# Four edits to the start and the MoE tails of a two-layer encoder kernel: surplus blocks in groups of five, v weights requested ahead of the gathers, first x tile and first weights loaded first, transposes inside the products

## The chip, the cores and the metric

One core of a Trainium2 chip runs the whole kernel. The metric is the device time of one execution in microseconds (us), the median over several executions. Engines are named PE (TensorE), DVE (VectorE), ACT (ScalarE), POOL (GpSimd) and SP (SyncE, which here only issues DMAs); "PEld" is the weight load that goes with each matmul.

## What is computed

Two post-norm layers over x of 512 tokens by 1024 columns, all in float32. Layer 0 mixes with retention and a gated recurrence, layer 1 with HGRN2 heads. After each mixer and after each mixture of experts (MoE) there is a layer norm.

```python
for layer in range(2):
    y = even_mixer(h) if layer == 0 else odd_mixer(h)
    h = layer_norm(ALPHA * h + y)
    y = moe(h)          # 16 experts, 4 groups; each token: best group, its top 2 experts
    h = layer_norm(ALPHA * h + y)
def expert(xb, e):
    return (silu(xb @ w_gate[e]) * (xb @ w_up[e])) @ w_down[e]
```

The reference is dropless: however many tokens choose an expert, all of them are served.

## The kernel before, in words

Every engine has its program written out by hand, and the engines meet at semaphores. A float32 matmul with 512 columns is two PE instructions in the profile.

**Start (layer 0, first input projection).** SP asks for the identity `sq`, then the four 128-token tiles of x (L282), the first 512 columns of `w_in_even` in two halves (L286, L287), and the other four groups (L289). PE runs four warming matmuls (`spin`), transposes the four tiles of x (`turn_h(0, t)`, L425; 8 transposes each), spins three more times, and waits for all of `hT`. ACT copies the transposed tiles to `hT` (L846) after it has issued its own loads, the last of them the retention decay table of 1.8 MB (L866). Then come 20 products `project(n)` (L460) of 16 instructions each. Products 0 to 3 multiply token tile n by the first weight group, so product n needs only tile n. DVE's first work is the rotary step of product 0 (L1105), which waits for all tables.

**MoE.** Each expert has 96 slots, which gives 12 units of 128 rows (`NU`); unit 11 is `LAST`. Tokens beyond 96 go to surplus blocks of 128 rows; their number `nx` comes out of the router (table entry `T_NX`) and can be 0 to 10 (`MAXX`). The weights of three experts are held at a time, in `W[0:12288]`, `W[12288:24576]` and `S[0:12288]`. The results of all units but the last go to DRAM (`slot_rows`). After the last unit each engine runs its surplus loop (PE L638, DVE L1431, ACT, SP):

```python
with pe.Fori(0, MAXX, 1) as j:
    with pe.If(j < nx):
        turn_rows(0, ...); gate_up_extra(...); turn_hidden(...); down_extra(...)
```

POOL gathers each token's two result rows back from DRAM once the last store has landed (L1578, 8 gathers of 128 rows into `Yg`). DVE adds them into `h` (L1253, L1255, the "merges", two per token tile), and PE adds the rows of the last unit in PSUM (L651 with the identity, L656 with a selection matrix, eight instructions per token tile). DVE then normalises tile by tile (L1227 to L1237, `standardise`). In layer 0 the first norm result is transposed (L425), and the v products of layer 1 follow (L702). Their weights, 4 MB, are asked for at L362 once the last up product is done, because they go to `W[12288:20480]`, where expert 14's weights lie. In layer 1 the output is stored after the norm.

Of the kernel before, what the change touches and what calls it, by code (L numbers as in the profile page):

```python
# [15 lines left out]
ALU = mybir.AluOpType  # L16
# [3 lines left out]
P = 128  # L20
# [16 lines left out]
LAST = NU - 1  # L37
ALPHA = float((2.0 * DEPTH) ** 0.25)
# [32 lines left out]
def encoder_kernel(nc, x, w_in_even, w_out_even, lru_conv_w, lru_conv_b, lru_gate_w, lru_gate_b,  # L71
# [3 lines left out]
    with ExitStack() as ctx:  # L75
# [68 lines left out]
        w_v1, w_out1 = W3(12288, ND, D), S3(0, ND, D)  # L144
# [20 lines left out]
        Yg = [S3(0, NT * 2, D), W3(12288, NT * 2, D)]  # L165
# [27 lines left out]
        T_NX, T_STORES, T_COPIES = 10, 11, 12  # L193
# [85 lines left out]
        def _(sp):  # L279
            sp.dma_start(sq[:], c_sq.rearrange("p (a n) -> p a n", a=3)).then_inc(sq_in, 16)  # L280
            for t in range(NT):
                sp.dma_start(h[:, t, :], x[0, t * P:(t + 1) * P, :]).then_inc(x_in[t], 16)  # L282
            for n, first in enumerate(W_GROUPS):
                src = w_in_even[0][:, first:first + 512].rearrange(rows, p=P)
                if n == 0:
                    sp.dma_start(w_grp[0][:, 0:4, :], src[:, 0:4, :]).then_inc(win_in[5], 16)  # L286
                    sp.dma_start(w_grp[0][:, 4:8, :], src[:, 4:8, :]).then_inc(win_in[0], 16)  # L287
                else:
                    sp.dma_start(w_grp[n], src).then_inc(win_in[n], 16)  # L289
            sp.dma_start(gate_w, lru_gate_w[0].rearrange("z g n c d -> c (z g n) d")).then_inc(gatew_in, 16)  # L290
# [43 lines left out]
            def moe_loads(L):  # L334
# [25 lines left out]
                if L == 0:  # L360
                    sp.wait_ge(up_mm[0], NU)
                    sp.dma_start(w_v1, w_in_odd[0][:, D:2 * D].rearrange(rows, p=P)).then_inc(wout_in, 16)  # L362
                sp.wait_ge(table_done, L + 1)
                nx = sp.value_load(tbl[0:1, T_NX:T_NX + 1], min_val=0, max_val=MAXX)
                with sp.Fori(0, MAXX, 1) as j:
                    with sp.If(j < nx):
                        e = sp.value_load(tbl[0:1, bass.ds(j, 1)], min_val=0, max_val=NE - 1)
                        sp.wait_ge(down_mm[L], (j + NU) * 2)
                        load_rows(L, j + NU, 0)
                        load_expert(L, e, 0)  # L370
# [21 lines left out]
            head_weights(0, 0)  # L392
            head_weights(1, 1)
            sp.wait_ge(v_ps, 2 * NT)
            sp.dma_start(masks, c_masks).then_inc(masks_in, 16)
# [20 lines left out]
        def _(pe):  # L416
            def turn_h(n, t):
# [5 lines left out]
                for half in range(2):  # L423
                    for c in range(4):
                        last = pe.transpose(ps[:, 2 * t + half, c * P:(c + 1) * P],  # L425
# [9 lines left out]
            spin(7, 4)  # L435
            for t in range(NT):
                turn_h(0, t)
            pe.wait_ge(hT_done, 2)
            spin(0, 3)
            pe.wait_ge(hT_done, 2 * NT)  # L440

            def project(n):
# [8 lines left out]
                elif n >= 4:  # L451
                    pe.wait_ge(proj_used, n - 3)
                for c in range(ND):
# [1184 lines left out]
```

## Time and profile before

| what | value |
|---|---|
| runs | 1399.14, 1404.2, 1405.28 us; median 1404.2 us |
| the profiled execution, its own time | 1403.62 us |
| its span | 1401.7 us |
| PE busy | 1349.4 us, 96% of the span |
| DVE, ACT, POOL busy | 518.4, 194.1, 166.7 us |
| mean granted PE clock | 0.986 of full |

The profiled execution lies 0.6 us below the median. "Busy" counts an engine's compute instructions and nothing that its sequencer does, so an engine in an empty loop shows as idle. The granted clock is given as a share of full speed: 1.00 is 2.4 GHz and 0.50 is 1.2 GHz. In the rows below "[5.26 <-DVE h L1255]" means that the engine had stood idle for 5.26 us, and what the profile takes to be the releaser.

### The profile page before, as it was taken

The page shows a single profiled execution, that of the slowest core. Times are in us where ns is not written, and L with a number is a line of the kernel's source. Part 1 is how long each engine was busy: PE and PEld are TensorE (multiplying, and loading weights), DVE is VectorE, ACT ScalarE, POOL GpSimd, SP SyncE. Part 2 cuts the span into 40 slices and gives each one's busy share as a digit, 9 for nine tenths or more (in the row PEclk, how much of TensorE's full clock was granted, in tenths as well). Part 3 has the DMA queues.
Part 4 walks back from the last instruction along what each step waited for, and adds up shares of the span by engine and source line. Part 5 has one row for each costly group of instructions (what it writes and reads, how often), then busy time and mean ns, then how long its engine had stood idle before and what let it go on. Part 6 is the DMA issues. An engine that isn't in the chain of part 4 may idle for free.

```text
span 1401.7 us, 16406 instructions
## 1 busy us (share of the span) xinstructions
PE 1349.4 (96%) x6751; PEld 612.8 (44%) x6751; DVE 518.4 (37%) x972; ACT 194.1 (14%) x327; POOL 166.7 (12%) x126
## 2 busy tenths in 40 slices
PE   8999999999999999799999999999999999999995
PEld 4444464633333333244455555555545333333322
DVE  1244763333111111430355666665545131111107
ACT  1025400100000001010211111111111000000000
POOL 0000400050000000200122332222201400000020
PEclk9999999999999999899999999999999999999998
DMA  9920165368999995633421122200085889999852
GB/s 348 353 85 1 45 255 209 155 233 298 408 424 403 425 414 232 249 90 97 127 61 30 31 60 60 60 0 0 21 369 214 295 336 424 406 427 408 372 213 88
DMA packets 82888, 305.75 MB, mean 218 GB/s; under 512 B 5444, under 2 KB 49800, under 8 KB 70408
## 3 DMA queue, kind: packets, MB, share of 16 engines
q1 hardware_dynamic: 61728, 262.81, 48.3%
q10 hardware_dynamic: 16488, 25.21, 4.9%
q0 software_dynamic: 4608, 16.78, 3.2%
q8 instruction: 52, 0.85, 0.2%
q14 instruction: 12, 0.10, 0.0%
HBM read 271.23 MB, written 33.55 MB: 217 GB/s over the span
## 4 chain that ended last, share of the span: by engine, by line
PE 86%; DVE 9%; issue 2%; ACT 1%; ACTq 1%; DVEq 1%
PE ps L559 24%; PE ps L715 13%; PE ps L594 11%; PE ps L460 8%; PE ps L517 7%; PE ps L702 4%; PE ps L737 3%; PE ps L767 2%; PE ps L544 2%; PE ps L509 1%; DVE S L1469 1%; PE ps L582 1%; PE ps L613 1%; PE ps L755 1%; PE ps L485 1%
## 5 line engine op out<-in xcount | busy, mean ns | idle before, releaser
L559 PE MATMUL ps<-W,S 128*32 128x512 f32 (+1 forms) x2048 | 336.7, 596 | 2.3 <-DVE S L1398 2.3
L715 PE MATMUL ps<-hT,W 128*128 128x512 f32 x512 | 232.5, 593 | 0.7 <-ACT W L846 0.7
L559 PE MATMUL ps<-S 128*64 128x512 f32 (+1 forms) x512 | 224.8, 597 | 0.4 <-DVE S L1398 0.4
L594 PE MATMUL ps<-W,hT 128*32 128x512 f32 (+1 forms) x1024 | 172.8, 601 | 1.1 <-DVE hT L1412 1.0
L559 PEld LDWEIGHTS ps<-W,S 128*32 128x32 f32 (+1 forms) x2048 | 97.8, 114 | 148.0 <-issue 143.7
L715 PEld LDWEIGHTS ps<-hT,W 128*128 128x128 f32 x512 | 92.8, 191 | 90.4 <-issue 88.5
L594 PE MATMUL ps<-S,hT 128*32 128x512 f32 (+1 forms) x256 | 113.2, 594 | 1.1 <-DVE hT L1412 1.0
L846 ACT ACTIVATE hT<-ps 128x512 f32<-128x512 f32 x82 | 46.6, 599 | 388.0 <-PE ps L594 287.0
L559 PEld LDWEIGHTS ps<-S 128*64 128x64 f32 (+1 forms) x512 | 62.1, 124 | 71.9 <-issue 70.5
L1600 POOL TENSOR_TENSOR W<-S,sq 128x256 f32<-128x256 f32 x64 | 73.6, 1150 | 160.9 <-PE ps L737 117.2
L460 PE MATMUL ps<-W,hT 128*128 128x512 f32 x192 | 83.0, 593 | 0.7 <-ACT hT L846 0.7
L594 PEld LDWEIGHTS ps<-W,hT 128*32 128x32 f32 (+1 forms) x1024 | 48.8, 114 | 71.5 <-issue 69.7
L1403 DVE TENSOR_TENSOR hT<-hT,ps 128x512 f32<-128x512 f32 x24 | 16.5, 688 | 159.4 <-ACT hT L959 159.4
L737 PEld LDWEIGHTS ps<-S,W 128*128 128x128 f32 x448 | 61.5, 192 | 30.7 <-issue 30.7
L1511 DVE TENSOR_TENSOR S<-S 128x512 f32<-128x512 f32 x64 | 47.8, 748 | 69.9 <-PE ps L737 58.1
L1408 DVE TENSOR_TENSOR hT<-hT,ps 128x512 f32<-128x512 f32 x24 | 16.5, 688 | 149.5 <-PE ps L559 149.5
L1412 DVE COPY hT<-ps 128x512 f32<-128x512 f32 x24 | 16.6, 691 | 137.9 <-PE ps L582 137.9
L737 PE MATMUL ps<-S,W 128*128 128x128 f32 x448 | 63.5, 285 | 1.4 <-issue 0.8
L517 PE MATMUL ps<-S 128*128 128x512 f32 x128 | 58.4, 601 | 1.0 <-DVE S L1447 1.0
L846 ACT ACTIVATE W<-ps 128x512 f32<-128x512 f32 x56 | 32.6, 597 | 174.3 <-PE ps L746 46.8
L460 PEld LDWEIGHTS ps<-W,hT 128*128 128x128 f32 x192 | 36.3, 190 | 46.3 <-issue 45.0
L517 PE MATMUL ps<-W,hT 128*128 128x512 f32 x128 | 55.7, 593 | 0.8 <-ACT hT L846 0.8
(233 smaller groups left out, 1360.9 us busy)
## 6 DMA issues: line engine op xcount, KB each, us to landing
W<-moe_w_gate SPq DMA_DIRECT2D x24, 2048.0 KB, 12.3
W<-moe_w_up SPq DMA_DIRECT2D x24, 2048.0 KB, 13.1
W<-moe_w_down SPq DMA_DIRECT2D x24, 2048.0 KB, 11.5
S<-moe_w_gate SPq DMA_DIRECT2D x8, 2048.0 KB, 13.3
S<-moe_w_up SPq DMA_DIRECT2D x8, 2048.0 KB, 14.2
S<-moe_w_down SPq DMA_DIRECT2D x8, 2048.0 KB, 16.9
W<-w_in_odd SPq DMA_DIRECT2D x32, 512.0 KB, 6.3
slot_rows<-S ACTq DMA_DIRECT2D x4, 2816.0 KB, 19.4
```

Source lines behind the costliest of these rows:

```text
L460: last = pe.matmul(ps[:, 4 + n % 4, :], a, b, start=(c == 0), stop=(c == ND - 1))
L517: last = pe.matmul(ps[:, k, :], srcT[:, c, t * P:(t + 1) * P], w[:, c, half * 512:(half + 1) * 512], start=(start and c == tiles[0]), stop ...
L544: last = pe.transpose(ps[:, 4 + half, c * P:(c + 1) * P], block[:, half * 4 + c:D:ND], ident)
L559: last = pe.matmul(ps[a:a + n, bank, :], xgT[:, c, a:a + n], w[L][slot_of(e)][:, c, :], start=(c == 0), stop=(c == ND - 1))
L594: last = pe.matmul(ps[a:a + n, 2 + half, :], hidT[:, c, a:a + n], wd[L][slot_of(e)][:, c, half * 512:(half + 1) * 512], start=(c == 0), st ...
L702: last = pe.matmul(ps[:, k, :], hT[:, c, t * P:(t + 1) * P], w_v1[:, c, (k % 2) * 512:(k % 2 + 1) * 512], start=(c == 0), stop=(c == ND - 1))
L715: last = pe.matmul(ps[:, f % 2, :], ring[slot][:, f, c, :], hT[:, c, :], start=(c == 0), stop=(c == ND - 1))
L737: last = pe.matmul(o, km[level % 2][:, c * P:(c + 1) * P], mixed(Q2, s, c * P, P), start=True, stop=True)
L767: last = pe.matmul(ps[:, 7, :], vh[:, j, :], attn[:, j, :], start=(j == 0), stop=(j == NT - 1))
L846: return nc.scalar.activation(o, i, ACT.Copy)
L1511: v.tensor_tensor(q, q, view(src, at + 1, [[2, n], [step - 1, 2], [0, s]]), ALU.mult).then_inc(updated, 1)
L1600: pool.tensor_tensor(view(km[level % 2], s, [[4 * s, m], [s, 2], [1, s]]), view(K2, s, [[4 * s, m], [T + s, 2], [1, s]]), view(ones, 0, [[ ...
```

## The change

1. The surplus blocks come in up to two groups (`ROUNDS`) of five (`PER_ROUND`). The table holds the number of groups that are needed: 0, 1 or 2. Each engine's loop goes twice over the groups, with one test per group, and inside it five times over the blocks with none. A group that is needed at all runs all five blocks.
2. The v weights go to `S[0:8192]`, where expert 13's gate and up weights lie, and are asked for after the up product of unit 10 rather than unit 11. The gathered rows of layer 0 move to the down part of `S` and to `W[0:4096]`. The masks of layer 1 are asked for a little earlier.
3. SP asks for x tile 0, then both halves of the first weights, then x tiles 1 to 3, then weight group 1, then the decay table (which leaves ACT's queue), then the rest.
4. PE spins once rather than seven times. The transposes of tiles 1 to 3 stand inside products 0 to 2, after their fifth of eight steps. DVE copies them to `hT` instead of ACT.

```diff
 NU = NE * CAP // P
 MAXX = 2 * T // (CAP + 1)
 LAST = NU - 1
+ROUNDS = 2
+PER_ROUND = MAXX // ROUNDS
 ALPHA = float((2.0 * DEPTH) ** 0.25)
 LN_EPS, RMS_EPS = 1e-5, 1e-6
 GELU_C = 2.0 * float(np.sqrt(2.0 / np.pi))
...
-        w_v1, w_out1 = W3(12288, ND, D), S3(0, ND, D)
+        w_v1, w_out1 = S3(0, ND, D), S3(0, ND, D)
...
-        Yg = [S3(0, NT * 2, D), W3(12288, NT * 2, D)]
+        Yg = [[S3(8192, NT, D), W3(0, NT, D)], [W3(12288, NT, D), W3(16384, NT, D)]]
...
-        T_NX, T_STORES, T_COPIES = 10, 11, 12
+        T_ROUNDS, T_STORES, T_COPIES = 10, 11, 12
...
+
+            def rows_in(t):
                 sp.dma_start(h[:, t, :], x[0, t * P:(t + 1) * P, :]).then_inc(x_in[t], 16)
+
+            rows_in(0)
             for n, first in enumerate(W_GROUPS):
                 src = w_in_even[0][:, first:first + 512].rearrange(rows, p=P)
                 if n == 0:
                     sp.dma_start(w_grp[0][:, 0:4, :], src[:, 0:4, :]).then_inc(win_in[5], 16)
                     sp.dma_start(w_grp[0][:, 4:8, :], src[:, 4:8, :]).then_inc(win_in[0], 16)
+                    for t in range(1, NT):
+                        rows_in(t)
                 else:
                     sp.dma_start(w_grp[n], src).then_inc(win_in[n], 16)
+                if n == 1:
+                    sp.dma_start(decay, c_decay).then_inc(tab_in, 16)
             sp.dma_start(gate_w, lru_gate_w[0].rearrange("z g n c d -> c (z g n) d")).then_inc(gatew_in, 16)
             sp.wait_ge(proj, 20)
             sp.dma_start(w_out0, w_out_even[0].rearrange(rows, p=P)).then_inc(wout_in, 16)
...
                 if L == 0:
-                    sp.wait_ge(up_mm[0], NU)
+                    sp.wait_ge(up_mm[0], LAST)
                     sp.dma_start(w_v1, w_in_odd[0][:, D:2 * D].rearrange(rows, p=P)).then_inc(wout_in, 16)
                 sp.wait_ge(table_done, L + 1)
-                nx = sp.value_load(tbl[0:1, T_NX:T_NX + 1], min_val=0, max_val=MAXX)
-                with sp.Fori(0, MAXX, 1) as j:
-                    with sp.If(j < nx):
-                        e = sp.value_load(tbl[0:1, bass.ds(j, 1)], min_val=0, max_val=NE - 1)
-                        sp.wait_ge(down_mm[L], (j + NU) * 2)
-                        load_rows(L, j + NU, 0)
-                        load_expert(L, e, 0)
+                rounds = sp.value_load(tbl[0:1, T_ROUNDS:T_ROUNDS + 1], min_val=0, max_val=ROUNDS)
+                with sp.Fori(0, ROUNDS, 1) as r:
+                    with sp.If(r < rounds):
+                        with sp.Fori(0, PER_ROUND, 1) as i:
+                            j = r * PER_ROUND + i
+                            e = sp.value_load(tbl[0:1, bass.ds(j, 1)], min_val=0, max_val=NE - 1)
+                            sp.wait_ge(down_mm[L], (j + NU) * 2)
+                            load_rows(L, j + NU, 0)
+                            load_expert(L, e, 0)
 
 
             sp.wait_ge(lru_done, 1)
...
             head_weights(0, 0)
+            sp.dma_start(masks, c_masks).then_inc(masks_in, 16)
             head_weights(1, 1)
             sp.wait_ge(v_ps, 2 * NT)
-            sp.dma_start(masks, c_masks).then_inc(masks_in, 16)
...
-                        last = pe.transpose(ps[:, 2 * t + half, c * P:(c + 1) * P],
+                        last = pe.transpose(ps[:, (2 * t + half) % (4 if n == 0 else 8), c * P:(c + 1) * P],
...
             pe.wait_ge(sq_in, 16)
-            spin(7, 4)
-            for t in range(NT):
-                turn_h(0, t)
-            pe.wait_ge(hT_done, 2)
-            spin(0, 3)
-            pe.wait_ge(hT_done, 2 * NT)
+            spin(7, 1)
+            turn_h(0, 0)
 
             def project(n):
 
...
                     pe.wait_ge(proj_used, n - 3)
+                if n < NT:
+                    pe.wait_ge(hT_done, 2 * n + 2)
                 for c in range(ND):
                     if n == 0 and c == 4:
                         pe.wait_ge(win_in[0], 16)
+                    if n < NT - 1 and c == 5:
+                        turn_h(0, n + 1)
...
                 pe.wait_ge(table_done, L + 1)
-                nx = pe.value_load(tbl[0:1, T_NX:T_NX + 1], min_val=0, max_val=MAXX)
+                rounds = pe.value_load(tbl[0:1, T_ROUNDS:T_ROUNDS + 1], min_val=0, max_val=ROUNDS)
                 copies = pe.value_load(tbl[0:1, T_COPIES:T_COPIES + 1], min_val=2 * NU, max_val=2 * (NU + MAXX))
                 turn_hidden(LAST)
                 down(LAST)
-                with pe.Fori(0, MAXX, 1) as j:
-                    with pe.If(j < nx):
-                        turn_rows(0, (j + NU // 3) * 16)
-                        gate_up_extra(j + NU, (j + NE // 2 + 1) * 16)
-                        turn_hidden(j + NU)
-                        down_extra(j + NU, (j + NE // 2 + 1) * 16)
+                with pe.Fori(0, ROUNDS, 1) as r:
+                    with pe.If(r < rounds):
+                        with pe.Fori(0, PER_ROUND, 1) as i:
+                            j = r * PER_ROUND + i
+                            turn_rows(0, (j + NU // 3) * 16)
+                            gate_up_extra(j + NU, (j + NE // 2 + 1) * 16)
+                            turn_hidden(j + NU)
+                            down_extra(j + NU, (j + NE // 2 + 1) * 16)
 
...
-            act.dma_start(decay, c_decay).then_inc(tab_in, 16)
-            for t in range(NT):
-                turn_copies(0, t)
...
+            for k in range(2 * NT):
+                dve.wait_ge(hT_ps, k + 1)
+                v.tensor_copy(hT[:, 4 * (k % 2):4 * (k % 2) + 4, (k // 2) * P:(k // 2 + 1) * P],
+                              ps[:, k % 4, :].rearrange("p (c n) -> p c n", c=4)).then_inc(hT_done, 1)
...
-                    done(v.scalar_tensor_tensor(h[:, t, :], Yg[L][:, 2 * t, :], gts[:, t, 0:1], h[:, t, :],
+                    done(v.scalar_tensor_tensor(h[:, t, :], Yg[L][t // 2][:, 2 * (t % 2), :], gts[:, t, 0:1], h[:, t, :],
-                    v.scalar_tensor_tensor(h[:, t, :], Yg[L][:, 2 * t + 1, :], gts[:, t, 1:2], h[:, t, :],
+                    v.scalar_tensor_tensor(h[:, t, :], Yg[L][t // 2][:, 2 * (t % 2) + 1, :], gts[:, t, 1:2], h[:, t, :],
...
-                v.tensor_copy(r_tb[0:1, T_NX:T_NX + 1], r_end[0:1, NE - 1:NE])
-                done(v.tensor_scalar(r_tb[0:1, T_STORES:T_STORES + 1], r_end[0:1, NE - 1:NE], float(NU // 2), 16.0,
-                                     ALU.add, ALU.mult))
-                done(v.tensor_scalar(r_tb[0:1, T_COPIES:T_COPIES + 1], r_end[0:1, NE - 1:NE], float(NU), 2.0,
-                                     ALU.add, ALU.mult))
+                extra, n = r_end[0:1, NE - 1:NE], r_tb[0:1, T_ROUNDS:T_ROUNDS + 1]
+                done(v.tensor_scalar(n, extra, 1.0, None, ALU.is_ge))
+                for k in range(1, ROUNDS):
+                    done(v.scalar_tensor_tensor(n, extra, float(k * PER_ROUND + 1), n, ALU.is_ge, ALU.add))
+                v.tensor_scalar(r_tb[0:1, T_STORES:T_STORES + 1], n, 16.0 * PER_ROUND, 16.0 * (NU // 2),
+                                ALU.mult, ALU.add)
+                done(v.tensor_scalar(r_tb[0:1, T_COPIES:T_COPIES + 1], n, 2.0 * PER_ROUND, 2.0 * NU,
+                                     ALU.mult, ALU.add))
...
-                        pool.indirect_dma_start(Yg[L][:, 2 * t + k, :], None, xs,
+                        pool.indirect_dma_start(Yg[L][t // 2][:, 2 * (t % 2) + k, :], None, xs,

```

The loops of ACT and DVE are rewritten in the same way as those of SP and PE, around the same calls.

**PE at the start.** The order of PE's instructions before (L432 `spin`, L425 transposes, L460 products):

```order
L432 MATMUL ps<-sq 128x384 [waits sq_in]
L432 MATMUL ps<-sq 128x384 x3
L425 MATMUL ps<-sq,h 128x128 [waits x_in_0]
L425 MATMUL ps<-sq,h 128x128 x7
...
L425 MATMUL ps<-sq,h 128x128 [waits x_in_3]
L425 MATMUL ps<-sq,h 128x128 x7
L432 MATMUL ps<-sq 128x384 [waits hT_copied]
L432 MATMUL ps<-sq 128x384 x2
L460 MATMUL ps<-W,hT 128x512 [waits win_in_5,hT_copied]
L460 MATMUL ps<-W,hT 128x512 x3
L460 MATMUL ps<-W,hT 128x512 [waits win_in_0]
```

And now (the same three are L443, L436 and L471):

```order
L443 MATMUL ps<-sq 128x384 [waits sq_in]
L436 MATMUL ps<-sq,h 128x128 [waits x_in_0]
L436 MATMUL ps<-sq,h 128x128 x3
L471 MATMUL ps<-W,hT 128x512 [waits hT_copied,win_in_5]
L471 MATMUL ps<-W,hT 128x512 x3
L471 MATMUL ps<-W,hT 128x512 [waits win_in_0]
L436 MATMUL ps<-sq,h 128x128 [waits x_in_1]
L436 MATMUL ps<-sq,h 128x128 x7
L471 MATMUL ps<-W,hT 128x512 x3
L471 MATMUL ps<-W,hT 128x512 [waits hT_copied]
```

The first product now waits for tile 0 of x alone, and the transposes of tile 1 stand in it. The list folds repeated rows, so a transposed tile is still eight transposes.

**SP at the start**, before:

```order
L280 DMA sq<-c_sq 128x384
L282 DMA h<-x 128x1024 x4
L286 DMA W<-w_in_even 128x4x512
L287 DMA W<-w_in_even 128x4x512
L289 DMA W<-w_in_even 128x8x512 x4
```

and now:

```order
L282 DMA sq<-c_sq 128x384
L285 DMA h<-x 128x1024
L291 DMA W<-w_in_even 128x4x512
L292 DMA W<-w_in_even 128x4x512
L285 DMA h<-x 128x1024 x3
L296 DMA W<-w_in_even 128x8x512
L298 DMA S<-c_decay 128x3584
L296 DMA W<-w_in_even 128x8x512 x3
```

The first weights have moved ahead of three tiles of x, and the decay table ahead of three weight groups.

**PE at the end of the MoE**, layer 0, before (L594 down product of the last unit, L638 and L639 the loop and its test, then the surplus block):

```order
L594 MATMUL ps<-W,hT 32x512 x31
L638 UNCONDITIONAL_BRANCH
L639 COMPARE_AND_BRANCH
L550 ISA
...
L639 UNCONDITIONAL_BRANCH
L638 REGISTER_ALU
L638 COMPARE_AND_BRANCH
```

and now:

```order
L605 MATMUL ps<-W,hT 32x512 x31
L649 UNCONDITIONAL_BRANCH
L650 COMPARE_AND_BRANCH
L651 UNCONDITIONAL_BRANCH
L651 ISA
...
L651 REGISTER_ALU
L651 COMPARE_AND_BRANCH
L650 UNCONDITIONAL_BRANCH
L649 REGISTER_ALU
L649 COMPARE_AND_BRANCH
L664 MATMUL ps<-h,sq 128x512 [waits rows_merged,first_rows_or_last_sel_copied]
```

The outer loop and its test are of the same form as before, but go round twice rather than ten times. The inner loop (L651) is reached only where the test holds.

## Rows read from the trace of the kernel before

**Rows 1.** Page, part 1: busy time by engine, share, instructions.

```profile
PE 1349.4 (96%) x6751; PEld 612.8 (44%) x6751; DVE 518.4 (37%) x972; ACT 194.1 (14%) x327; POOL 166.7 (12%) x126
```

**Rows 2.** Timeline of the start: start us, length us, engine, line, operation, count.

```profile
3.25 4.42 PE L432 MATMUL ps<-sq 128*128 128x384 f32 x8 [3.25 <-DMA sq<-c_sq]
7.51 3.29 PE L425 MATMUL ps<-sq,h 128*128 128x128 f32 x24
12.18 4.03 ACT L846 ACTIVATE hT<-ps 128x512 f32<-128x512 f32 x8
16.26 27.73 PE L460 MATMUL ps<-W,hT 128*128 128x512 f32 x64 [0.74 <-ACT hT L846]
25.68 0.43 DVE L1105 TENSOR_TENSOR S<-S,rot 128x256 f32<-128x256 f32 x1 [25.68 <-DMA S<-c_decay]
```

**Rows 3.** Chain of waits, a later `spin` with PE at full clock: start us, length us.

```profile
268.50 3.32 PE ps L432 x10
```

**Rows 4.** Line 286 (first half of the first weights): issue, and time to landing.

```profile
L286 SPq DMA_DIRECT2D W<-w_in_even x1: 580/580/580, 3.0 to 3.0; - x1
DMA to landing us min/median/max: 11.3/11.3/11.3
```

**Rows 5.** SP's DMA queue (packets, MB, share), in windows 0 to 8 and 0 to 12.6 us.

```profile
q1 hardware_dynamic: 566, 1.77, 68.5%
q1 hardware_dynamic: 1239, 3.34, 76.3%
```

**Rows 6.** Page, part 6: every load of MoE gate weights.

```profile
W<-moe_w_gate SPq DMA_DIRECT2D x24, 2048.0 KB, 12.3
S<-moe_w_gate SPq DMA_DIRECT2D x8, 2048.0 KB, 13.3
```

**Rows 7.** Timeline of PE, DVE and POOL around layer 0's last unit.

```profile
568.83 8.77 PE L594 MATMUL ps<-W,hT 128*32 128x512 f32 x64 [0.98 <-DVE hT L1412]
582.87 3.75 PE L651 MATMUL ps<-h,sq 128*128 128x512 f32 x4 [5.26 <-DVE h L1255]
600.46 7.10 PE L702 MATMUL ps<-W,hT 128*128 128x512 f32 x16 [0.83 <-ACT hT L846]
...
576.79 1.28 DVE L1253 SCALAR_TENSOR_TENSOR h<-S,gts,h 128x1024 f32<-128x1024 f32 x1 [8.21 <-issue]
586.79 1.28 DVE L1253 SCALAR_TENSOR_TENSOR h<-S,gts,h 128x1024 f32<-128x1024 f32 x1 [2.35 <-DMA S<-slot_rows,dst]
...
562.76 1.03 POOL L1578 DMA_INDIRECT S<-slot_rows,dst  x1 [250.14 <-DMA slot_rows<-hT]
```

**Rows 8.** Chain in the same place: steps of DVE's sequencer in its empty loop.

```profile
571.38 0.71 issue
...
575.29 0.06 DVEq L1432
...
575.82 0.06 DVEq L1432
```

**Rows 9.** Timeline of SP: the issue ahead of the v weights' in its program.

```profile
544.84 0.43 SPq L298 DMA_DIRECT2D S<-ln_b  x1
```

**Rows 10.** Timeline of PE, DVE and POOL around layer 1's last unit.

```profile
1374.44 3.75 PE L651 MATMUL ps<-h,sq 128*128 128x512 f32 x4 [6.13 <-issue]
...
1367.82 1.28 DVE L1253 SCALAR_TENSOR_TENSOR h<-W,gts,h 128x1024 f32<-128x1024 f32 x1 [8.42 <-issue]
1380.22 1.30 DVE L1227 BATCH_NORM_STATS2 sm<-ps 128x6 f32<-128x512 f32 x2 [2.25 <-PE ps L656]
...
1354.81 1.03 POOL L1578 DMA_INDIRECT W<-slot_rows,dst  x1 [249.12 <-DMA slot_rows<-hT]
```

**Rows 11.** Gathers of layer 1: GB/s in 40 slices of 1356 to 1370 us.

```profile
GB/s 0 117 105 105 234 410 433 304 339 328 386 363 374 433 363 199 281 222 328 316 328 339 281 363 339 316 316 351 398 398 339 398 421 433 421 386 316 222 23 0
```

**Rows 12.** Stretches: length, busy us (instructions) of PE, PEld, DVE, ACT, POOL; granted clock; DMA share; GB/s.

```profile
568.80:577.60 8.80, 8.77 (x64) 2.85 (x64) 0.81 (x1) 0.60 (x1) 2.87 (x4) 0.81 1.02 401
582.80:586.60 3.80, 3.73 (x5) 1.70 (x6) 1.60 (x2) 1.28 (x1) 0.00 (x0) 0.50 0.94 376
```

More of the change, by code:

```diff
@@ L865, in _ @@
             act.dma_start(iota[:], c_iota).then_inc(tab_in, 16)
-            act.dma_start(decay, c_decay).then_inc(tab_in, 16)
-            for t in range(NT):
-                turn_copies(0, t)
             def projected(n):
@@ L985, in moe @@
                 act.wait_ge(table_done, L + 1)
-                nx = act.value_load(tbl[0:1, T_NX:T_NX + 1], min_val=0, max_val=MAXX)
-                with act.Fori(0, MAXX, 1) as j:
-                    with act.If(j < nx):
-                        sigmoid(j + NU)
-                        store(j + NU, 0, (j + NU // 2) * 16)
+                rounds = act.value_load(tbl[0:1, T_ROUNDS:T_ROUNDS + 1], min_val=0, max_val=ROUNDS)
+                with act.Fori(0, ROUNDS, 1) as r:
+                    with act.If(r < rounds):
+                        with act.Fori(0, PER_ROUND, 1) as i:
+                            j = r * PER_ROUND + i
+                            sigmoid(j + NU)
+                            store(j + NU, 0, (j + NU // 2) * 16)
             norm_std(0, 0)
@@ L1429, in moe @@
                 dve.wait_ge(table_done, L + 1)
-                nx = dve.value_load(tbl[0:1, T_NX:T_NX + 1], min_val=0, max_val=MAXX)
-                with dve.Fori(0, MAXX, 1) as j:
-                    with dve.If(j < nx):
-                        copy_rows(j + NU)
-                        hidden(j + NU)
-                        copy_hidden(j + NU)
+                rounds = dve.value_load(tbl[0:1, T_ROUNDS:T_ROUNDS + 1], min_val=0, max_val=ROUNDS)
+                with dve.Fori(0, ROUNDS, 1) as r:
+                    with dve.If(r < rounds):
+                        with dve.Fori(0, PER_ROUND, 1) as i:
+                            j = r * PER_ROUND + i
+                            copy_rows(j + NU)
+                            hidden(j + NU)
+                            copy_hidden(j + NU)
             norm_mixer(0)
```

## Prediction

> **What bounds the kernel now.** I began with the busy times: PE computes for 1349.4 of 1401.7 us [rows 1], so all that a change outside PE's own instructions can reach is some 52 us of PE idle time, plus stretches in which PE runs at half clock. The waits, in order of time, put that idle time in a few places. The change touches three of them: the start, and the end of the MoE in each layer. So I read the timeline there.
>
> *Start.* PE's first product begins at 16.26 us, released by ACT's last copy [rows 2]. ACT copies only from 12.18 us, because its own loads stand ahead on its queue. The first half of the weights, which the same product needs, was asked for at 3.05 us and landed 11.3 us later, at 14.35 [rows 4]. So both releasers are within 2 us of each other: a faster copy alone would gain little, and the order of the loads matters.
>
> *End of layer 0's MoE.* The last down product ends at 568.83 + 8.77 = 577.6 us; PE then stands idle for 5.26 us [rows 7]. The profile names DVE's merge as the releaser, but DVE merged tile 0 from 576.79 to 579.4, long before 582.87. What is left is PE's own empty loop. DVE's loop shows what a round costs: its sequencer passes the same line at 575.29 and 575.82, 0.53 us a round [rows 8], and ten rounds are 5.3 us, which is PE's whole gap. Layer 1 shows 6.13 us there [rows 10].
>
> *No surplus block runs.* There are 24 + 8 = 32 loads of gate weights [rows 6], which is 16 experts times 2 layers. Every round of the loops is an empty one.
>
> **The change part by part.**
>
> *Loops.* Ten empty rounds become two of the same form, so 8 x 0.53 = 4.2 us go on PE, and as much on DVE, ACT and SP. In layer 0 PE's gap falls from 5.3 to 1.1 us, and its sums may begin at 578.7 rather than 582.87. What could hold them is the merge. DVE's idle time before its merges was 8.21 us [rows 7]; less 4.2 it is 4.0, so they begin at about 572.6 and take 2.6 us a tile. Tile 0 is merged at 575.2, before PE asks. In layer 1 PE's gap falls from 6.1 to 1.9 us and the merges begin at 1367.82 - 4.2 = 1363.6 [rows 10].
>
> *Clock.* The long gap costs twice. In it the granted clock fell to 0.50, that is 1.2 GHz, and stayed there for the first 3.8 us of the sums [rows 12]: the first tile's eight instructions took 5.4 us, where eight at full clock take 3.4 (27.73 / 64 = 0.43 us each, rows of the products [rows 2]). With a gap of 1.1 us it may stay at 2.4 GHz. The evidence is mixed: gaps of 1.48 and 0.98 us close together brought it to 0.81 on the mean of the down product that followed [rows 12], in layer 1 nothing of the kind shows. So layer 0 gains 4.2 us (clock falls all the same) to 6.1 us (it holds). I take **5.5**.
>
> *Layer 1's end.* PE's last product ends at 1374.44 - 6.13 = 1368.3, and the first sum is ready 5.8 us after PE's start, at 1380.22, which is what DVE's norm waits for [rows 10]; the rest is DVE's chain of four norms, unchanged. After the change the sum begins at 1370.2 and is ready at 1373.6 (full clock) to 1375.9 (half). DVE must have merged all four tiles first: four times 2.6 us from 1363.6 are 1373.8. The gathers bound this too. They begin at 1354.81 and their traffic ends at 1369.3 [rows 10, 11]; with a landing lag of 1.75 us (below) tile 3 is merged at 1373.7. So the norm begins between 1373.8 and 1375.9, a gain of 4.3 to 6.4 us. I take **5.5**, nearer to the full clock since the gap of 1.9 us is nearer to those that hardly lowered it than to 6.1. This is also why faster loops alone can't give more: DVE and the gathers stand right behind.
>
> *v weights earlier.* In layer 0 DVE waited 2.35 us for tile 3's rows, until 586.79 [rows 7], with the v weights on the same DMA engines (share 1.02 [rows 12]). With PE's sums moved up, tile 3's sum would be due at 578.7 + 3 x 3.44 = 589.0, and the merge ended at 589.4; the norm of tile 0, behind that merge on DVE, would end 1.4 us after PE's last sum. Asked for at about 545.3, behind the issue at 544.84 [rows 9], the weights are nearly through when the gathers begin at 562.8, and these then take as long as in layer 1, to about 579. So this edit is worth 0 to 1.4 us, and only because of the first; it is within the 5.5. What it may hurt is queued on the same engines: the last down weights, due at 568.8, and the store of unit 10 before the gathers. 2.1 + 1.0 + 4.2 + 0.5 MB at the 401 GB/s of [rows 12] are 19.5 us, until 564.5, so the store may land 2 to 3 us later. The last merge moves to 585 at most, before 589.0: no cost. The masks, the new places and one more small DVE operation in the table lie beside PE work and are not waited for: nothing.
>
> *Start.* SP's queue had moved 1.77 MB by 8.0 us and 3.34 MB by 12.6 [rows 5]. Before, the first half of the weights had the identity and all of x ahead of it, 0.2 + 2.1 + 1.05 = 3.34 MB; it landed at 14.35, so the lag is 1.75 us. Now it has 0.2 + 0.52 + 1.05 = 1.77 MB and lands at 8.0 + 1.75 = **9.75 us**. Tile 0's transposes and DVE's two copies are done before. The second half and tiles 1 to 3 follow at 0.34 MB a us: 12.9, 14.4, 16, 17.5, each before its use. So the products begin 6.5 us earlier. Two things are given back. The transposes of three tiles now stand on PE's path: 3.29 us for 24 [rows 2]. And the warming goes: the first eight spin instructions took 4.42 us, 0.55 each [rows 2], where ten later ones took 3.32 [rows 3], so PE starts at half rate here. (The clock row says 1.00 at the start, but the durations decide.) One spin and one tile of transposes with idle time between will hardly raise it before 9.75; then the first product pays what the first sum paid, 2.1 us. The gain is 6.5 - 3.3 - 2.1 = **1.1 us**; bounds: 4.0 (weights at 9.0 and full clock) and -1.0 (a tile or half of the weights 2 us late).
>
> The Trainium skill ("TensorE: Matmul & The Clock Gate", part 1) speaks against this edit: PE's default clock is the low one, and work issued before it has been busy for a while runs at half rate, however few instructions it is. By that page the removed spins were no waste, and the start gains 1.1 us rather than 3.2. The durations above agree.
>
> The decay table lands later than DVE's first rotary step at 25.68 us [rows 2], by some 3 us, but PE needs the rotated rows only after product 7, at about 70 us.
>
> **Sum.** 1.1 + 5.5 + 5.5 = 12.1 us off the profiled execution's 1403.6, which is 1391.5; that execution lies 0.6 us under the median, so 1392.0.
>
> **The rivals.**
>
> *The loops' time is not by the round.* DVE's gap of 8.2 us is more than 5.3: four or five steps took 0.7 us each [rows 8], and they may be a fixed price of entering and leaving the loop that PE pays as well. For it: layer 1's gap on PE is 6.1. Against it: layer 0's is 5.3, ten rounds exactly. Then PE's gap falls only to some 3 us, the clock falls too, and each layer gains 2.3: 1404.2 - 1.1 - 4.6 = 1398.5.
> The Trainium skill ("Runtime: NRT & Kernel Launch", Instruction fetch mechanics) says that a taken branch to code outside the fetched window stalls until it is fetched. By it such steps belong to jumps, not to rounds, and would stay; no row here tells which it is.
>
> *All goes well at once.* The start keeps full clock, both first sums too, and the gathers come early: 4.0 + 7 + 7 = 18 us, 1386.
>
> *Slower: groups of five.* A layer with one surplus block now runs five. Place: the end of that MoE, PE's path. Price: a block has 16 + 16 + 16 product instructions at 0.43 us, 21 us, so four needless blocks cost at least 83 us: 1475 or more. It decides as soon as one expert is chosen by more than 96 tokens. [Rows 6] speak against it flatly: neither layer has a surplus block.
>
> **How the numbers follow.** Forecast 0.68 (own range 1388 to 1396); fixed loop price 0.15; all at once 0.13; groups of five 0.02; something else near no change 0.02. 0.5% is 7.0 us, about what a measurement can tell from no change: below 1397.2 is faster. That is the forecast, all at once and a third of the fixed-price case: 0.86. Same takes the rest of that case, 0.12. Slower 0.02. The range runs from 1386 to 1398: both bounds of the unknowns added up give 4.0 + 6.1 + 6.4 = 16.5 and -1.0 + 4.2 + 4.3 = 7.5 us, and 1386 and 1398 take in part of the two rivals.
>
> **What would show it.** First product at 9 to 10.5 us, its first instructions near 0.86 us apart, product 3 ended near 42.6 rather than 43.8. PE idle 1 to 2 us before the identity sums in both layers, granted clock 1.00 in the first sum. v products from 594 to 596. Layer 1's first norm at about 1368 us, 12 earlier than 1380.2. No DMA wait before DVE's last merge. I am wrong if PE's gaps stay over 3 us, if the products at the start wait for tiles of x, or if gathers become the releaser of PE's sums.

## The result, and the profile after the change

The changed kernel takes 1386.85 us in the median (1386.09 to 1388.84, 4 runs), against 1404.14 us before (1399.14 to 1405.28). The ratio is 0.9886, with a 95% interval of 0.986 to 0.9912: 17.3 us, or 1.1%, faster. The prediction said 1392.0 with a range of 1386 to 1398, so the direction is right, the step is 1.4 times the forecast one (17.3 against 12.1 us), and the time lies near the low end of the range. The profiled execution took 1388.84 us, the slowest of the four; its span is 1387.0 us, 14.7 less than before.

PE's own work has hardly changed (page, part 1; compare [rows 1]):

```profile
PE 1346.3 (97%) x6739; PEld 613.2 (44%) x6739; DVE 524.5 (38%) x982; ACT 189.9 (14%) x319; POOL 167.2 (12%) x126
```

*The start.* PE's timeline there, which answers to [rows 2]:

```profile
3.19 1.65 PE L443 MATMUL ps<-sq 128*128 128x384 f32 x2 [3.19 <-DMA sq<-c_sq]
5.34 1.97 PE L436 MATMUL ps<-sq,h 128*128 128x128 f32 x8 [0.50 <-DMA h<-x]
8.57 6.68 PE L471 MATMUL ps<-W,hT 128*128 128x512 f32 x10 [1.25 <-DMA W<-w_in_even]
15.09 1.04 PE L436 MATMUL ps<-sq,h 128*128 128x128 f32 x8
40.95 27.68 PE L471 MATMUL ps<-hT,W 128*128 128x512 f32 x64
```

The first product begins at 8.57 us, released by the weights, and its first ten instructions take until 15.09. At full clock ten take 4.3 us, so the half rate costs 2.2. The granted-clock column reads 1.00 for this stretch, as it did at the start before the change; that PE is at half rate is read from the durations, and the warm start below bears it out. No transpose inside a product waits for x. The second group of products begins at 40.95 us (before: 43.90).

*The end of layer 0's MoE*, PE, POOL and DVE, which answers to [rows 7]:

```profile
565.25 8.77 PE L605 MATMUL ps<-W,hT 128*32 128x512 f32 x64 [0.98 <-DVE hT L1431]
573.95 1.98 PE L664 MATMUL ps<-h,sq 128*128 128x512 f32 x4
589.65 7.11 PE L715 MATMUL ps<-S,hT 128*128 128x512 f32 x16 [0.83 <-ACT hT L859]
...
563.86 1.03 POOL L1599 DMA_INDIRECT S<-slot_rows,dst  x1 [251.18 <-DMA slot_rows<-hT]
...
570.78 1.28 DVE L1269 SCALAR_TENSOR_TENSOR h<-S,gts,h 128x1024 f32<-128x1024 f32 x1 [5.78 <-DMA S<-slot_rows,dst]
```

PE's gap of 5.26 us is gone: the identity sum follows the last down product at once. DVE is through its loop early and now waits for the gathered rows. The granted clock is 0.80 in the down product and 1.00 in the first sum.

*The end of layer 1's MoE*, PE and DVE, which answers to [rows 10]; the last three lines are from the chain of waits:

```profile
1359.71 1.98 PE L664 MATMUL ps<-h,sq 128*128 128x512 f32 x4
...
1354.17 1.29 DVE L1269 SCALAR_TENSOR_TENSOR h<-W,gts,h 128x1024 f32<-128x1024 f32 x1 [1.72 <-DMA W<-slot_rows,dst]
1365.57 1.29 DVE L1243 BATCH_NORM_STATS2 sm<-ps 128x6 f32<-128x512 f32 x2
...
1356.59 6.44 DMA W<-slot_rows,dst
1363.03 0.03 issue
1363.05 1.30 DVE h L1269
```

Here too PE's gap is gone. What ends last now is POOL's eighth gather (6.44 us from issue to landing), then tile 3's merge, then the norms. Before, PE's empty loop stood in that place.

The difference of the two profiled executions, summed up from the start of the same instruction in both:

| place | before | after | gained since the start |
|---|---|---|---|
| second product group begins | 43.90 | 40.95 | 2.95 |
| retention finished, out projection begins | 204.66 | 203.37 | 1.29 |
| layer 0, first-row selection | 289.86 | 288.58 | 1.28 |
| layer 0, last up product | 558.55 | 555.58 | 2.97 |
| v products begin | 600.46 | 589.65 | 10.81 |
| layer 1, first-row selection | 1082.99 | 1074.34 | 8.65 |
| layer 1, DVE behind the last up product | 1357.18 | 1350.23 | 6.95 |
| last norm begins | 1380.22 | 1365.57 | 14.65 |

So the three places that the change touches gave 2.95, 7.84 (10.81 - 2.97) and 7.70 us (14.65 - 6.95), 18.5 in all. The stretches in between, which it does not touch, lost 3.8 us net: 1.7 before the out projection, 2.2 and 1.7 on either side of layer 1's first-row selection, while layer 0's MoE gained 1.7. PE's instructions there are the same. The mean granted clock is 0.01 lower in the three that lost and 0.01 higher in the one that gained, and PE's busy time moves with it (from 43.90 to 204.66 us before, 158.28 us; the same work after, 159.95 us).

### The profile page after: what moved, and what is told of

The parts are those of the page before. It is cut to its first block, busy times and chain, and to the rows that moved or that the text cites. A ratio compares the mean times of both kernels' runs of the same rounds, so it can differ in the third digit from the quotient of the medians.

```text
span 1387.0 us, 16128 instructions
## 1 busy us (share of the span) xinstructions
PE 1346.3 (97%) x6739; PEld 613.2 (44%) x6739; DVE 524.5 (38%) x982; ACT 189.9 (14%) x319; POOL 167.2 (12%) x126
## 4 chain that ended last, share of the span: by engine, by line
PE 88%; DVE 8%; DMA 1%; issue 1%; ACT 1%; POOL 0%; DVEq 0%; POOLq 0%; SPq 0%
PE ps L570 24%; PE ps L728 14%; PE ps L605 12%; PE ps L471 8%; PE ps L528 7%; PE ps L715 4%; PE ps L750 4%; PE ps L780 2%; PE ps L555 2%; PE ps L443 1%; PE ps L520 1%; DVE S L1490 1%; PE ps L593 1%; PE ps L624 1%; PE ps L768 1%
## 5 line engine op out<-in xcount | busy, mean ns | idle before, releaser
L859 ACT ACTIVATE hT<-ps 128x512 f32<-128x512 f32 x74 | 42.5, 596 | 385.9 <-PE ps L605 287.0
L471 PE MATMUL ps<-W,hT 128*128 128x512 f32 x192 | 85.6, 605 | 1.3 <-DMA W<-w_in_even 1.3
L1532 DVE TENSOR_TENSOR S<-S 128x512 f32<-128x512 f32 x64 | 47.8, 747 | 69.9 <-PE ps L750 58.0
L471 PEld LDWEIGHTS ps<-W,hT 128*128 128x128 f32 x192 | 36.9, 195 | 46.5 <-issue 44.8
L715 PE MATMUL ps<-S,hT 128*128 128x512 f32 x128 | 55.7, 593 | 0.8 <-ACT hT L859 0.8
## 6 DMA issues: line engine op xcount, KB each, us to landing
W<-moe_w_gate SPq DMA_DIRECT2D x24, 2048.0 KB, 12.6
```

The costliest lines, as they stand in the source:

```text
L471: last = pe.matmul(ps[:, 4 + n % 4, :], a, b, start=(c == 0), stop=(c == ND - 1))
L715: last = pe.matmul(ps[:, k, :], hT[:, c, t * P:(t + 1) * P], w_v1[:, c, (k % 2) * 512:(k % 2 + 1) * 512], start=(c == 0), stop=(c == ND - 1))
L859: return nc.scalar.activation(o, i, ACT.Copy)
L1532: v.tensor_tensor(q, q, view(src, at + 1, [[2, n], [step - 1, 2], [0, s]]), ALU.mult).then_inc(updated, 1)
```

## The experiments

Each kernel was run beside the kernel before. The theory: an empty round costs every engine 0.53 us, and nothing else; the loads' order and the transposes inside the products need each other; the early v weights matter little. Its rivals: a fixed price of the loops; a single edit that carries the start; v weights that matter.

**Ten groups of one block.**

```diff
-ROUNDS = 2
+ROUNDS = 10
```

> The changed kernel with ten groups of one block, so each empty loop goes round ten times again; all else as changed. If the price is by the round (0.53 us), PE stands idle 5 to 6 us before its identity sums in both layers, the clock falls in that gap, and each layer's end is 6 to 8 us longer than in the changed kernel: 1386.9 + 14 = about 1401. If the price is that of entering and leaving a loop, PE's gap stays near nothing and the time within 2 us of 1387.

Measured: 1397.14 us (1394.55 to 1398.68), ratio 0.9963 (0.9949 to 0.9977). That is 10 us more than the changed kernel, and its gaps are back. PE and DVE at both ends:

```profile
567.07 7.07 PE L605 MATMUL ps<-W,hT 128*32 128x512 f32 x64 [0.98 <-DVE hT L1431]
579.02 3.46 PE L664 MATMUL ps<-h,sq 128*128 128x512 f32 x4 [4.88 <-DVE h L1271]
...
1368.23 3.75 PE L664 MATMUL ps<-h,sq 128*128 128x512 f32 x4 [5.20 <-issue]
1361.10 1.28 DVE L1269 SCALAR_TENSOR_TENSOR h<-W,gts,h 128x1024 f32<-128x1024 f32 x1 [5.39 <-issue]
```

The price is by the round: PE stands for 4.88 and 5.20 us, and the first sum runs at the low clock again (granted 0.53 and 0.50 in it). In layer 0 the profile names DVE's merge as the releaser, but that had ended at 576.03. DVE's 5.39 us in layer 1 are ten rounds at 0.53 with no slow step among them, so a round and its jump can pass without the slow steps of [rows 8]; this nested loop is other code than the loop before, so what brings them is not shown. Entering and leaving the loop is the same here as in the changed kernel, so the rival of a fixed price is out. The total was expected 4 us higher. Layer 1's end is 6.0 us longer than in the changed kernel, as expected; layer 0's, from the last up product to the v products, only 4.7 (38.81 against 34.07), because part of the gap takes the place of time that the changed kernel loses there too: 1.7 us to a low clock in the down product, or 1.7 us of waiting for the first rows (last experiment).

**The two groups of five alone, in the kernel before.** The table of the groups and the loops are taken over, nothing else; for example on PE:

```diff
-                with pe.Fori(0, MAXX, 1) as j:
-                    with pe.If(j < nx):
+                with pe.Fori(0, ROUNDS, 1) as r:
+                    with pe.If(r < rounds):
+                        with pe.Fori(0, PER_ROUND, 1) as i:
```

> The kernel before with the two groups of five alone. By the round: PE's gaps of 5.3 and 6.1 us vanish; layer 1's end gains what it gained in the changed kernel (7.7 us), layer 0's a little less than its 7.8, since the v weights still share the DMA engines with the gathers and DVE's last merge is late: 1404.1 - 14 = 1390, give or take 2 for the clock. Fixed price: 1402 or more.

Measured: 1396.2 us (1393.79 to 1397.01), ratio 0.9952 (0.9938 to 0.9965). Half of what was expected. PE's gaps at the loop are gone, except for 0.65 us in layer 0, but in layer 0 PE now waits for the merges of tiles 1 to 3, and each of these for its gather:

```profile
575.32 1.95 PE L657 MATMUL ps<-h,sq 128*128 128x512 f32 x4 [0.65 <-issue]
579.96 1.98 PE L657 MATMUL ps<-h,sq 128*128 128x512 f32 x4 [0.97 <-DVE h L1263]
585.36 1.98 PE L657 MATMUL ps<-h,sq 128*128 128x512 f32 x4 [1.70 <-DVE h L1263]
590.73 1.98 PE L657 MATMUL ps<-h,sq 128*128 128x512 f32 x4 [1.67 <-DVE h L1263]
...
577.30 1.28 DVE L1261 SCALAR_TENSOR_TENSOR h<-S,gts,h 128x1024 f32<-128x1024 f32 x1 [4.94 <-DMA S<-slot_rows,dst]
588.07 1.29 DVE L1261 SCALAR_TENSOR_TENSOR h<-S,gts,h 128x1024 f32<-128x1024 f32 x1 [2.76 <-DMA S<-slot_rows,dst]
```

Tiles come 5.4 us apart while the v weights share the DMA engines. The faster loop turned one wait into another: from the last up product to the v products it is 39.31 us, only 2.6 less than before. Layer 1's end gained 5.1 us rather than 7.7; in this one profile its last store took 5.5 us to land, with nothing large beside it (DMA share 0.28), and the gathers began that much later. Why is open.

**The changed kernel with late v weights.**

```diff
-                    sp.wait_ge(up_mm[0], LAST)
+                    sp.wait_ge(up_mm[0], NU)
```

> The changed kernel with the v weights asked for after the last up product again, at their new place. If their early start matters now that the loops are short: the gathers of layer 0 take 20 us or more from the first to the last merge's rows instead of 15, the sums or the first transposes behind them wait, and the v products begin 1 to 4 us later against the end of the last down product; 1388 to 1391. If other work hides it: no DMA wait that PE sees, under 0.5 us.

Measured: 1391.33 us (1389.46 to 1393.49), ratio 0.9926 (0.9901 to 0.9952), 4.5 us slower than the changed kernel (on another chip; by the ratios to the kernel before it is 0.4%, 5.6 us). PE's sums and the v products:

```profile
574.90 1.98 PE L664 MATMUL ps<-h,sq 128*128 128x512 f32 x4
578.44 1.88 PE L664 MATMUL ps<-h,sq 128*128 128x512 f32 x4
583.68 1.98 PE L664 MATMUL ps<-h,sq 128*128 128x512 f32 x4 [1.65 <-DVE h L1271]
589.04 1.98 PE L664 MATMUL ps<-h,sq 128*128 128x512 f32 x4 [1.66 <-DVE h L1271]
595.54 7.10 PE L715 MATMUL ps<-S,hT 128*128 128x512 f32 x16 [0.83 <-ACT hT L859]
```

From the first sum to the v products it takes 20.6 us here and 15.7 in the changed kernel: 4.9 us. The first gather, at 560.76 us, is earlier than there, but tile 3's rows come 25.6 us after it, where the changed kernel has them within 15 to 16. The early request is worth that, not the 0 to 1.4 us of the prediction.

**One group of ten.**

```diff
-ROUNDS = 2
+ROUNDS = 1
```

> The changed kernel with one group of ten blocks, so one empty round. If PE's two rounds are already hidden behind the last down product in the array, and DVE waits for gathered rows, nothing is left to gain: gaps as in the changed kernel, 1387 within 2. If each round still shows, 0.5 us less in each layer.

Measured: 1388.62 us (1384.9 to 1389.34), ratio 0.9898 (0.9864 to 0.9932): no difference to the changed kernel. PE's sum in layer 1 begins at once, in layer 0 it waits 1.38 us for DVE's merge, whose rows are late. Two rounds are as good as one: with two, no gap is left on PE that the rounds make.

**The start: x first.**

```diff
-            rows_in(0)
+            for t in range(NT):
+                rows_in(t)
...
-                    for t in range(1, NT):
-                        rows_in(t)
...
-                if n == 1:
-                    sp.dma_start(decay, c_decay).then_inc(tab_in, 16)
...
+            act.dma_start(decay, c_decay).then_inc(tab_in, 16)
```

> The changed kernel with the loads in the old order: all four tiles of x before the weights, the decay table on ACT's queue. If the order of the loads carries the gain at the start: the first product begins at about 14.4 us (where the first half of the weights landed before) and product 3 ends near 46.5, because the transposes stand inside the products and the clock is low; that is 5 to 6 us later than in the changed kernel (40.9) and later than before the change (43.8): about 1392. If moving the transposes and the copies to DVE carries it, product 3 ends by 42.

Measured: 1391.62 us (1390.42 to 1395.19), ratio 0.993 (0.9902 to 0.9957). The first product and the one that ends the first group:

```profile
14.35 6.33 PE L468 MATMUL ps<-W,hT 128*128 128x512 f32 x10 [7.30 <-DMA W<-w_in_even]
...
36.88 9.61 PE L468 MATMUL ps<-W,hT 128*128 128x512 f32 x22
```

It begins at 14.35 us, as expected from [rows 4], and product 3 ends near 46.3, 2.5 us later than before the change. Transposes inside the products, with the spins gone, are a loss by themselves. Most of it is the half rate: the first ten instructions take 6.33 us where 4.3 would do.

**The start: transposes first.**

```diff
-            spin(7, 1)
-            turn_h(0, 0)
+            spin(7, 4)
+            for t in range(NT):
+                if t >= 2:
+                    pe.wait_ge(hT_done, 2 * t - 2)
+                turn_h(0, t)
+            pe.wait_ge(hT_done, 2 * NT)
...
-                    if n < NT - 1 and c == 5:
-                        turn_h(0, n + 1)
```

> The changed kernel with its new order of loads, but four spins and all four transposed tiles ahead of the first product again. If both edits are needed together: tile 3 of x lands at about 16, the first product begins at 18 to 19 and product 3 ends at 45 to 47; about 1392. If the new order of loads alone gives the gain, product 3 ends by 42.

Measured: 1395.08 us (1392.43 to 1399.69), ratio 0.9953 (0.9931 to 0.9975).

```profile
14.07 5.38 PE L436 MATMUL ps<-sq,h 128*128 128x128 f32 x24 [4.12 <-DMA h<-x]
20.24 26.02 PE L473 MATMUL ps<-W,hT 128*128 128x512 f32 x60 [0.78 <-DVE hT L1112]
```

PE waits for tile 1 until 14.07, and the first product begins at 20.24, later than the expected 18 to 19. There is no further wait for x; the 24 transposes behind tile 1 take 5.38 us at a granted clock of 0.50, where 24 took 3.29 before [rows 2]. Product 3 ends at 47.8. The weights ahead of x are a loss by themselves too. Only the pair gains.

**A warm start.**

```diff
-            spin(7, 1)
+            spin(7, 2)
             turn_h(0, 0)
+            spin(7, 1)
```

> The changed kernel with two spins before the first transposes and one behind them, so PE is hardly idle from 3.2 us to the first product. If the 2.1 us lost in the first product (ten instructions in 6.4 us) are the low clock, and it can be raised by then: the first product begins at 8.6 to 9.2 and product 3 ends 1 to 2 us earlier than 40.9; the total gains as much, within the noise of 1387. If the clock stays low whatever is spun, product 3 ends at 40.9 to 41.5.

Measured: 1385.35 us (1384.59 to 1386.27), ratio 0.9875 (0.9851 to 0.9899). The total is within the noise of the changed kernel, the profile is not:

```profile
10.11 4.56 PE L472 MATMUL ps<-W,hT 128*128 128x512 f32 x10 [2.17 <-DMA W<-w_in_even]
```

Ten instructions in 4.56 us where the changed kernel took 6.68: the removed spins had been worth 2.1 us. The expectation still missed: the weights landed 1.5 us later in this execution, so the first product did not begin by 9.2, and product 3 ended at 40.5, hardly before 40.9.

**A warm start, and spins in the wait at the retention scores.**

```diff
             scores(0)
             pe.wait_ge(proj_used, 16)
+            spin(7, 7)
```

> As the one before, and with seven spins in PE's wait of 2.5 us between the first and second head's retention scores, where the clock fell and PE's instructions up to 186 us took 1.7 us longer in the changed kernel than before the change. If idle time lowers the clock there: granted clock 1.00 in that stretch and 1.5 to 3 us off, 1383 to 1385 in all. If the clock falls for another reason: no gain, or a loss of up to 0.5 us where the spins outlast the wait.

Measured: 1382.95 us (1380.37 to 1384.53), ratio 0.9859 (0.9831 to 0.9886). The stretch of 165 to 190 us, first of the changed kernel in its second profile (last experiment), then of this one:

```profile
165.00:190.00 25.00, 22.53 (x64) 11.98 (x62) 16.70 (x24) 2.08 (x3) 1.54 (x1) 0.80 0.84 342
```

```profile
165.00:190.00 25.00, 25.00 (x107) 14.95 (x107) 18.36 (x40) 2.09 (x3) 0.00 (x0) 1.00 0.94 387
```

The granted clock (third from the right) is 1.00 where it was 0.80. In the eleven profiles without these spins, the kernel before included, it is 0.80 or 0.86 in this stretch. So here idle time lowers it, and the idle time can be filled. Seven spins took 4.78 us in a wait of 2.5, so they outlasted it by about 2 us.

**The v weights ahead of the last down weights**, in the changed kernel: the same request, moved up in SP's program to just behind unit 10's up product.

```diff
+                        if L == 0 and u == LAST - 1:
+                            sp.wait_ge(up_mm[0], LAST)
+                            sp.dma_start(w_v1, ...).then_inc(wout_in, 16)
                         next_down(L, q + 3, q)
```

> The changed kernel with the v weights asked for still earlier, as soon as unit 10's up product is done, ahead of expert 15's down weights and the norm's rows. If the slow landing of unit 10's store (7.5 us against 3.5 with the v weights late) is due to those weights on the same DMA engines: the store lands in about 3.5 us and layer 0's first gather begins 3 to 4 us earlier against the last down product. PE's sum then waits for no merge; the total gains 0 to 1.8 us (nothing where the down product ran at the low clock, as in the changed kernel's profile). If the store is slow for another reason: still 7 to 8 us.

Measured: 1384.94 us (1383.58 to 1385.2), ratio 0.9879 (0.9853 to 0.9904). The store of unit 10 and the first gather that waits for it:

```profile
556.49 0.34 ACTq L979 DMA_DIRECT2D slot_rows<-hT  x1
559.97 1.03 POOL L1599 DMA_INDIRECT S<-slot_rows,dst  x1 [248.47 <-DMA slot_rows<-hT]
```

In the changed kernel the same two are

```profile
556.32 0.34 ACTq L979 DMA_DIRECT2D slot_rows<-hT  x1
...
563.86 1.03 POOL L1599 DMA_INDIRECT S<-slot_rows,dst  x1 [251.18 <-DMA slot_rows<-hT]
```

That is 3.48 us here against 7.5 there (8.2 in its second profile). So the v weights, asked for where the change put them, do delay the store by 4 us. Asked for at 533.07 us they land 12.7 us later instead of 22.9, and the store finds the engines at a share of 0.32 (556 to 560 us). PE's sum waits for no merge, though the down product ran at full clock. The median is 2.3 us below that of the changed kernel on the same chip, and the ranges do not overlap.

**Both, with shorter spins.** The last kernel with the warm start, three spins at the scores and one in each of the two short gaps:

```diff
+                spin(4, 1)
                 turn_hidden(LAST)
+                spin(4, 1)
                 down(LAST)
```

> As the one before, with the spins at the start (two and one), three spins in the wait at the retention scores, and one spin in each of the two short gaps ahead of the last down product. If idle gaps lower the clock and the spins fit into them: last down product 7.1 us in both layers, first scores without a dip, no gap before the sums; 1379 to 1382. If the spins in the short gaps delay the down product instead: 1383 or more.

Measured: 1377.73 us (1377.2 to 1383.32), ratio 0.9842 (0.9814 to 0.987), the fastest median of all and below the expected 1379 to 1382: 9.5 us under the changed kernel on the same chip. Its slowest run, 1383.32, is still faster than every run of that. The last down product and the sum of layer 0:

```profile
559.20 7.07 PE L607 MATMUL ps<-W,hT 128*32 128x512 f32 x64 [0.33 <-DVE hT L1435]
566.20 1.98 PE L668 MATMUL ps<-h,sq 128*128 128x512 f32 x4
```

Neither the low clock nor a gap before the sum. The clock in 165 to 190 us is 1.00 here as well, with PE's second scores begun 2.2 us earlier than with seven spins.

**The changed kernel once more**, on the chip of the last two.

> The changed kernel itself, beside the two others on the same chip: 1385 to 1389, ratio to the kernel before 0.986 to 0.990. Its profile tells how much of the clock's dips in the places that the change does not touch differ from one execution to the next; if they do not differ, they follow from the change and not from chance.

Measured: 1387.27 us (1385.31 to 1389.52), ratio 0.9894 (0.987 to 0.9918). In this second profile the first product begins at 9.85 us, the second group at 42.48, and layer 0's last down product takes 7.07 us rather than 8.77 (granted clock 1.00 rather than 0.80). PE then waits for DVE's first merge:

```profile
575.11 1.96 PE L664 MATMUL ps<-h,sq 128*128 128x512 f32 x4 [1.73 <-DVE h L1271]
```

So the end of layer 0's MoE is no shorter for it: 34.23 us from the last up product to the v products, 34.07 in the first profile. The stretch at 165 to 190 us has clock 0.80 as in the first profile. So part of the dips differs from one execution to the next and part comes back each time.

## Why the prediction was right, and where its sizes were off

*Loops.* Right in mechanism: with ten groups PE's gaps of 5 us are back. Mis-sized in two terms. The first: I let the two rounds that remain cost 1.1 us in layer 0 and left a gap of 1.9 us in layer 1. No gap is left in either ("1359.71 ... L664" has none before it). Why the remaining rounds don't show is open; that they run in PE's sequencer while the array still works would fit, but is not shown. The second: of layer 0's 5.5 us the loops were to bring most. With the loops alone (second experiment) that end gained 2.6 us, since the wait for the loop became a wait for rows.

*Clock behind the gap.* Right: the first sum of four instructions takes 1.98 us where it took 3.75, in both layers, at a granted clock of 1.00 where it was 0.50. The shorter gap was worth about 2 us besides the gap itself, in each.

*v weights.* The step that failed is "this edit is worth 0 to 1.4 us". It measured 4.9 us in the profile and 4.5 in the total. I had compared the old landing of tile 3 with sums that began a microsecond late, and had not seen that with the loop shortened PE's sums of the later tiles would each wait for their own gather. So the 7.8 us of layer 0's end, against 5.5 taken, hold two errors of opposite sign: the loops gave less, the v weights more. The cost side was closer: the store was said to land 2 to 3 us later, and landed 4 us later. The prediction called that harmless. It is so only where the last down product runs at the low clock. In the second profile, where it did not, PE waited 1.73 us, and in the runs with one group, with the warm start and with the seven spins 1.4 to 1.8. That is the prediction's own sign of being wrong, gathers as what PE's sums wait for: it showed there, and not in the first profile.

*Layer 1's end.* Taken 5.5 us, bounds 4.3 to 6.4; it gave 7.7, and 8.1 in the second profile, so both lie outside the bounds. The gathers bind, as said, but DVE began its merges at 1354.17, 1.72 us behind its last copy, while I had left it 4.2 us of loop and slow steps. So it was never late, and the norm began 18.2 us after the first gather rather than 19 to 21.

*Start.* Taken 1.1 us; the first profile gave 2.95 and the second 1.4 (43.90 to 42.48). The second group began between 40.73 and 42.77 us in the six profiles with this start, and at 43.90 and 43.27 in the two with the old one. The term that differs most is the landing of the weights: products from 9.75 us predicted, from 8.57 in the first profile, 9.85 in the second. The three tiles of transposes cost 2.6 us rather than 3.3 (15.09 to 15.96 us for the first of them). The low clock's 2.1 us are as predicted (2.2), and the warm start got them back. The Trainium skill ("TensorE: Matmul & The Clock Gate", part 1) says that the throttled clock is PE's default and that activity releases it. The runs agree: ten instructions took 6.68 us behind one spin and 4.56 behind three.

*Rivals.* The fixed price of the loops is refuted by the ten groups. No surplus group ran in any execution, so the price of groups of five was not tried. "All goes well at once", put at 0.13, is nearer to the time (1386) than the forecast (1392), and two of its three parts happened: both ends gave over 7 us with the first sums at full clock. Its start did not: that kept the low clock.

*The sum.* 1.1 + 5.5 + 5.5 = 12.1 us predicted against 17.3 measured in the medians. The three places gave 18.5 us in the profiled execution (17.2 in the second profile), and the stretches elsewhere took 3.8 back (1.4). The time lies inside the stated range, 1386 to 1398, but outside the range of the forecast itself, 1388 to 1396. That it is inside owes something to the room left for the rivals, since each of the three terms was too small.

## What to carry to other kernels

An empty round of a guarded loop is not free: where several engines run ten of them behind the last product, it made the two longest waits of PE in this program (6.13 and 5.26 us), and grouping the rounds removed them. Before you shorten a wait, look up which transfer stands right behind it, and request ahead of it whatever shares its DMA engines, early enough that it has landed by then. Two edits that each lose by themselves may gain together (the load order and the place of the transposes), so undo each alone before you judge one. Where PE's clock falls in a wait of 1 to 2.5 us, as here, spins that are no longer than the wait can keep it up.

## What the runs showed of the hardware that was not expected

- Layer 0's last 0.5 MB store landed in 3.5 us with the v weights asked for late or very early, and in 7.5 to 8.3 us while they were under way, although it came from another queue (DMA share 0.96 from 556 to 564 us in the changed kernel). Quiet engines are no guarantee: layer 1's took 3.5 to 5.5 us. Gathers of 0.5 MB each that share with a 4 MB load bring a tile of two every 5.4 us.
- Slow steps of 0.7 us in DVE's empty loop [rows 8] were there in both layers before, and not in layer 1 with ten groups (5.39 us for ten rounds). What causes them is open.
- The same kernel's last down product took 8.77 us in one profile and 7.07 in another, after nearly the same gaps (0.87 or 0.86, and 0.98 us).
- The landing of the first weights varied between 8.5 and 10.1 us after the start of the program over kernels that ask for them in the same order.
